# Sample rows of the six token-major units as fp32 products with the raw weights, in four groups of 32 weight columns

## What is computed

```python
h = _rmsnorm(x, norm_g)                       # (tokens, 1024)
proj = jnp.einsum('btd,de->bte', h, w_in)     # w_in is (1024, 4608)
qa, ka, va, ga, xb, gb, qc, kc, vc, gc = jnp.split(proj, SPLIT_IDX, axis=-1)
oa, s_new = _retention(qa, ka, va, s0)        # 4 heads, chunks of 128 tokens
ob, h_new, conv_new = _rglru(xb, ...)         # width-4 convolution, then a linear recurrence
oc = attention(rmsnorm(qc), rmsnorm(kc), vc)  # window of 128, sample rows against a cache
mixed = concat[rmsnorm(oa) * silu(ga), ob * silu(gb), oc * silu(gc)]
y = x + mixed @ w_out                         # w_out is (1536, 1024)
```

## Time and profile before

| | |
|---|---|
| median of the runs | 698.38 us (3 runs, 698.27 to 698.42) |
| the profiled execution | 698.62 us |
| its span, first to last instruction | 696.8 us |
| mean granted clock of TensorE | 1.000 |
| PE busy | 688.7 us, 99% |
| PEld busy | 667.9 us, 96% |
| DVE busy | 291.9 us, 42% |
| ACT busy | 264.6 us, 38% |
| POOL busy | 106.1 us, 15% |
| DMA engines | 78 GB/s over the span |

### The profile page before, as it was taken

The page is one execution under the profiler, slowest core; times in us unless marked ns, Lnnn a source line. Parts: engine busy times, 40 slices in busy tenths (PEclk is TensorE's granted clock), DMA queues, the critical chain, the costliest instruction groups (busy, mean ns, idle before and its releaser), DMA issues.

```text
span 696.8 us, 11812 instructions
## 1 busy us (share of the span) xinstructions
PE 688.7 (99%) x4662; PEld 667.9 (96%) x4662; DVE 291.9 (42%) x645; ACT 264.6 (38%) x656; POOL 106.1 (15%) x231
## 2 busy tenths in 40 slices
PE   8999999999999999999999999999999999999998
PEld 8999999999999999999999999899899999999998
DVE  6311452343335439875532465227533662500000
ACT  7473242323232353667526554335543560200000
POOL 0002260535353000000002321122100000000000
PEclk9999999999999999999999999999999999999999
DMA  8912105122121211101041010121001351522220
GB/s 302 390 44 92 61 2 211 32 66 61 64 62 58 79 51 60 40 23 61 1 145 67 11 62 1 72 75 62 1 1 61 122 182 32 166 75 64 65 65 35
DMA packets 28146, 54.41 MB, mean 78 GB/s; under 512 B 2520, under 2 KB 20440, under 8 KB 25884
## 3 DMA queue, kind: packets, MB, share of 16 engines
q1 hardware_dynamic: 28092, 53.65, 22.9%
HBM read 46.56 MB, written 9.12 MB: 80 GB/s over the span
## 4 chain that ended last, share of the span: by engine, by line
PE 95%; ACT 1%; DVE 1%; DMA 1%; issue 1%; POOL 0%; SPq 0%; DVEq 0%
PE proj L417 22%; PE proj L419 21%; PE proj L418 21%; PE branch L419 4%; PE branch L418 4%; PE branch L417 4%; PE branch L588 2%; PE branch L653 2%; PE branch L630 2%; PE branch L504 1%; PE branch L521 1%; PE branch L536 1%; PE branch L542 1%; PE branch L643 1%; PE branch L524 1%; DMA mixed<-x_T 1%
## 5 line engine op out<-in xcount | busy, mean ns | idle before, releaser
L417 PE MATMUL proj<-big 128*128 128x352 f32 (+1 forms) x952 | 305.7, 321 | 1.9 <-DVE big L1147 1.9
L418 PE MATMUL proj<-big 128*128 128x352 f32 (+1 forms) x952 | 290.7, 305 | 0.0
L419 PE MATMUL proj<-big 128*128 128x352 f32 (+1 forms) x952 | 290.7, 305 | 0.0
L417 PEld LDWEIGHTS proj<-big 128*128 128x128 f32 x952 | 179.3, 188 | 5.7 <-ACT big L811 2.3
L418 PEld LDWEIGHTS proj<-big 128*128 128x128 f32 x952 | 179.4, 188 | 2.6 <-issue 1.9
L419 PEld LDWEIGHTS proj<-big 128*128 128x128 f32 x952 | 179.3, 188 | 0.0
L1142 DVE TENSOR_TENSOR big<-raw,big 128x512 fp32r<-128x512 f32 x72 | 48.8, 690 | 64.6 <-ACT big L805 64.6
L1570 POOL TENSOR_SCALAR stat<-stat 128x1 f32<-128x1 f32 (+2 forms) x68 | 18.0, 264 | 278.6 <-ACT junk L933 189.3
L419 PE MATMUL branch<-m_hi,big 128*128 128x352 f32 x180 | 58.0, 322 | 0.0
L418 PE MATMUL branch<-m_lo,big 128*128 128x352 f32 x180 | 58.0, 322 | 0.0
L417 PE MATMUL branch<-m_hi,big 128*128 128x352 f32 x180 | 57.9, 322 | 0.0
(11 more groups left out here) (219 smaller groups left out, 943.0 us busy)
## 6 DMA issues: line engine op xcount, KB each, us to landing
raw<-w_units SPq DMA_DIRECT2D x17, 1024.0 KB, 4.9
mixed<-x_T SPq DMA_DIRECT2D x12, 352.0 KB, 7.6
xy<-x_T SPq DMA_DIRECT2D x24, 176.0 KB, 2.4
out_y_T<-xy SPq DMA_DIRECT2D x24, 176.0 KB, 1.9
raw<-w_out SPq DMA_DIRECT2D x6, 512.0 KB, 4.1
xy<-w_out SPq DMA_DIRECT2D x6, 512.0 KB, 4.3
mixed<-x_prompt SPq DMA_DIRECT2D x5, 512.0 KB, 14.1
s<-state_ret SPq DMA_DIRECT2D x4, 512.0 KB, 3.9
```

The source lines that it names most:

```text
L417: pe.matmul(out, a_lo, b_hi, start=first, stop=False)
L418: pe.matmul(out, a_hi, b_lo, start=False, stop=False)
L419: return pe.matmul(out, a_hi, b_hi, start=False, stop=last)
```

## The change

The sample group of the six token-major units is computed in another way.

- `sample_rows(u)`, at the start of unit u: eight fp32 products, one for each k block, of the 32 sample tokens (`h_s`, the sum of the two parts) with the raw weights (`raw`). Block k goes to weight columns 32g to 32g + 31 of the array with g = k mod 4, and so to partitions 32g to 32g + 31 of `bb[4]`; the bank then holds four partial sums.
- ACT copies the bank to `hold` (`hold_copy`), ahead of slot 0.
- `sample_sum(u, out)`, where the last half of the sample group was: one fp32 product of 128 rows by 32 columns with four identities of 32 one below the other (`ident_32`, later a copy of it in `st_T[:, 0, :]`), which adds the four parts into the group's bank.
- `h_samp`, `sample_pass`, `fold_copy` and DVE's addition are gone. DVE makes `h_s` once, behind the splits of unit 1.
- `raw` is read until `sample_rows(u)` is done, so `load_w(u + 1)` waits for it (`pre_done`), and in token-major units `w_at` is (6, 8, 10, 12) in place of (3, 5, 7, 9). `load_w(16)` moves behind the loads of the second half's cache.
- Users of `bb[4]` wait for `held`; `sample_rows` of units 13 and 15 wait for the tails and for the end of the sample attention of half 0 (`smix_c`, DVE L1452, slot 15 of unit 14).

```diff
--- before.py
+++ after.py
@@ -61,7 +61,7 @@
     return NT + 1 if UNITS[u][0] in TOKEN_MAJOR else 6
 
 
-FOLDS = [u for u in range(NU) if UNITS[u][0] in TOKEN_MAJOR]
+TOKEN_UNITS = [u for u in range(NU) if UNITS[u][0] in TOKEN_MAJOR]
 FIRST_GROUP = [sum(n_groups(v) for v in range(u)) for u in range(NU + 1)]
 GROUPS = [(u, j) for u in range(NU) for j in range(n_groups(u))]
 
@@ -126,7 +126,8 @@
             return big[:, a + part * D:a + (part + 1) * D]
 
 
-        h_samp = sb("h_samp", [P, KD, 2 * NS], F32R)
+        h_s = sb("h_s", [P, KD, NS])
+        hold = sb("hold", [P, UNIT])
         raw = sb("raw", [P, wsz])
         ident = sb("ident", [P, P])
         ones = sb("ones", [P, P])
@@ -168,13 +169,13 @@
             o_sq = sb("o_sq", [P, P], scope=r)
             o_rs = sb("o_rs", [P, 2, NS], scope=r)
             erow = sb("erow", [P, NS], scope=r)
+            ident_32 = sb("ident_32", [P, 32], scope=r)
         with ExitStack() as r:
 
             sb("mixed_s", [P, 3 * H, TOK], scope=r)
             sb("under_v", [P, 2 * (NT + 1) * UNIT + N_CR], scope=r)
             xt = sb("xt", [P, 3, D], scope=r)
             dgs = sb("dgs", [P, NT + 1, 32], scope=r)
-            ident_32 = sb("ident_32", [P, 32], scope=r)
         with ExitStack() as r:
             sb("mixed_b", [P, 3 * H, TOK], scope=r)
             XW = 3 + SEQ + DB * 7
@@ -216,8 +217,8 @@
             w0_in0 w0_in1 w0_in2 w0_in3 x_in0 x_in1 x_in2 x_in3 x_in4 x_in5 x_in6 x_in7 x_in8 x_in9 x_in10 x_in11
             xt_in0 xt_in1 xt_in2 xt_in3 xt_in4 xt_in5 xt_in6 xt_in7 xt_in8 x_again0 x_again1 x_again2 wo_in0 wo_in1 wo_in2 wo_in3
             stored_cache stored_ret stored_tails stored_kv stored_y0 stored_y1 stored_y2
-            ones_set h_hi_set h_lo_set hs_set sq_set e9_set rcol_set ecol_set diag_set spread rb_set
-            row_set gate_set ga_set ga_silu w_hi_set w_lo_set proj_done act_freed fold_set folded
+            ones_set h_hi_set h_lo_set hs_set pre_done held sq_set e9_set rcol_set ecol_set diag_set spread rb_set
+            row_set gate_set ga_set ga_silu w_hi_set w_lo_set proj_done act_freed
             scores_done kturn_done masked kdec_set qdec_set vsel_set o_done kv_done kv2_done s_set s2_set
             o_ss o_pow o_ms o_root o_set oT_done mix_a
             lam_exp decay_set conv_set gates_done gates_read exp_set m2_set m_set
@@ -269,6 +270,8 @@
                 if u > 0:
                     sp.wait_ge(S_["w_hi_set"], PIECES * u)
                     sp.wait_ge(S_["w_lo_set"], PIECES * u)
+                if u - 1 in TOKEN_UNITS:
+                    sp.wait_ge(S_["pre_done"], TOKEN_UNITS.index(u - 1) + 1)
                 sp.dma_start(raw[:], io["w_units"][u]).then_inc(S_["raw_in"], 16)
 
             def load_cache(half):
@@ -328,6 +331,7 @@
             for u in range(9, 13):
                 load_w(u)
             sp.wait_ge(S_["lru_set"], H)
+            sp.dma_start(st_T[:, 0, :], io["c_ident_32"]).then_inc(S_["ident_32_in"], 16)
             sp.dma_start(cc[:], io["c_att"][:, 0:N_CC]).then_inc(S_["cc_in"], 16)
             load_cache(0)
             load_w(13)
@@ -343,6 +347,7 @@
                     sp.dma_start(cc[:, C_BIAS:N_CC], io["c_att"][:, N_CC:N_CC + 4 * P]).then_inc(S_["cc_in"], 16)
                     sp.wait_ge(S_["sav_done"], 1)
                     load_cache(1)
+                    load_w(16)
 
                 for t in (NT - 1, NT):
                     n9 = 9 * half + t
@@ -356,8 +361,6 @@
                         store(io["s_k"][b, WINDOW - DS:WINDOW, half], kn[rows, n9 % 2, :], "stored_kv")
                         store(io["s_v"][b, WINDOW - DS:WINDOW, half], v_c[rows, half, t, :], "stored_kv")
                 load_w(15 + 2 * half)
-                if half == 0:
-                    load_w(16)
 
             sp.wait_ge(S_["w_hi_set"], PIECES * NU)
             sp.wait_ge(S_["w_lo_set"], PIECES * NU)
@@ -394,7 +397,8 @@
         SILU_AT = {(7, 3): 0, (7, 4): 1, (10, 4): 2, (10, 5): 3, (12, 4): 4, (12, 5): 5, (12, 6): 6, (12, 7): 7}
 
         def w_at(u):
-            return (2, 3, 4, 5) if u == 7 else (0, 1, 2, 3) if 8 <= u <= 11 else (3, 5, 7, 9)
+            return (2, 3, 4, 5) if u == 7 else (0, 1, 2, 3) if 8 <= u <= 11 else \
+                (6, 8, 10, 12) if u in TOKEN_UNITS else (3, 5, 7, 9)
 
         def att_slot(u, s):
 
@@ -418,15 +422,28 @@
                 pe.matmul(out, a_hi, b_lo, start=False, stop=False)
                 return pe.matmul(out, a_hi, b_hi, start=False, stop=last)
 
-            def sample_pass(out, a, b_hi, b_lo, first, last):
-
-
-                if first:
-                    pe.matmul(out[0:2 * NS, :], a, b_hi, start=True, stop=False)
-                mm = pe.matmul(out[0:NS, :], a[:, 0:NS], b_lo, start=False, stop=False)
-                if not first:
-                    mm = pe.matmul(out[0:2 * NS, :], a, b_hi, start=False, stop=last)
-                return mm
+            def sample_rows(u):
+
+                pe.wait_ge(S_["raw_in"], 16 * u)
+                if u == TOKEN_UNITS[0]:
+                    pe.wait_ge(S_["hs_set"], 1)
+                if u == TOKEN_UNITS[3]:
+                    pe.wait_ge(S_["tails_copied"], 1)
+                if u == TOKEN_UNITS[5]:
+                    pe.wait_ge(S_["smix_c"], 1)
+                for k in range(KD):
+                    g = k % 4
+                    mm = pe.matmul(bb[4][32 * g:32 * g + NS, 0:UNIT], h_s[:, k, :], raw[:, k * UNIT:(k + 1) * UNIT],
+                                   start=(k < 4), stop=(k >= 4))
+                mm.then_inc(S_["pre_done"], 1)
+
+            def sample_sum(u, out):
+
+                i = TOKEN_UNITS.index(u)
+                if i in (0, 2):
+                    pe.wait_ge(S_["ident_32_in"], 16 if i == 0 else 32)
+                pe.wait_ge(S_["held"], i + 1)
+                return pe.matmul(out, ident_32[:] if i < 2 else st_T[:, 0, :], hold[:], start=True, stop=True)
 
             def first_unit():
                 pe.wait_ge(S_["ones_set"], 1)
@@ -455,6 +472,7 @@
             def spread_scale():
 
                 pe.wait_ge(S_["diag_set"], 1)
+                pe.wait_ge(S_["held"], 1)
                 for r in range(4):
                     rows = slice(32 * r, 32 * r + 32)
                     pe.matmul(bb[1 + r][:, 0:32 * NT], ones[rows, :], dgs[rows, 0:NT, :].rearrange("p t n -> p (t n)"),
@@ -477,7 +495,8 @@
                         cols = chunk_cols(j)
                         w = [w_part(u % 2, i)[:, k * UNIT:(k + 1) * UNIT] for i in range(2)]
                         if j == NT:
-                            mm = sample_pass(bank[:, 0:UNIT], h_samp[:, k, :], w[0], w[1], k == 0, k == KD - 1)
+                            if k == KD - 1:
+                                mm = sample_sum(u, bank[0:NS, 0:UNIT])
                             continue
                         mm = three_pass(bank[0:n, 0:UNIT], h_hi[:, k, cols], h_lo[:, k, cols], w[0], w[1],
                                         k == 0, k == KD - 1)
@@ -560,6 +579,8 @@
                     pe.wait_ge(S_["o_set"], m + 1)
                     if m > 0:
                         pe.wait_ge(S_["mix_a"], m)
+                    if m == 0:
+                        pe.wait_ge(S_["held"], 2)
                     pe.transpose(bb[4][:, 0:P], o_nrm[:, m % 2, :], ident[:]).then_inc(S_["oT_done"], 1)
                 else:
                     pe.wait_ge(S_["o_ss"], m + 1)
@@ -591,6 +612,7 @@
             def turn_tails():
                 pe.wait_ge(S_["lru_set"], H)
                 pe.wait_ge(S_["gates_read"], 24)
+                pe.wait_ge(S_["held"], 3)
                 for f in range(H):
                     mm = pe.transpose(bb[4][0:36, f * P:(f + 1) * P], tails[:, f, :], ident[:])
                 mm.then_inc(S_["tails_turned"], 1)
@@ -662,6 +684,7 @@
             def samp_scores(half, part):
 
                 if part == 0:
+                    pe.wait_ge(S_["held"], 5 + half)
                     pe.wait_ge(S_["qT_set"], 9 * half + 9)
                     pe.wait_ge(S_["kcache_in"], 16 * (half + 1))
                     if half == 0:
@@ -734,8 +757,6 @@
                         ret_one(base + s)
                 if (u, s) == (2, 3):
                     spread_scale()
-                if (u, s) == (2, 15):
-                    pe.wait_ge(S_["hs_set"], 2)
                 if (u, s) in LRU_AT["gates"]:
                     lru_gates(LRU_AT["gates"][u, s])
                 if (u, s) == TAILS_AT:
@@ -750,6 +771,8 @@
 
             first_unit()
             for u in range(1, NU):
+                if u in TOKEN_UNITS:
+                    sample_rows(u)
                 for j in range(n_groups(u)):
                     for half in range(2):
                         group_half(u, j, half)
@@ -837,16 +860,12 @@
                 bank = proj_bank(FIRST_GROUP[16] + e)
                 act.activation(bank[:, 0:CH], bank[:, 0:CH], ACT.Silu).then_inc(S_["ga_silu"], 1)
 
-            def fold_copy(u):
-
```

(33 more changed lines are left out.)

## The result

The changed kernel takes 702.33 us (median; five executions from 702.06 to 703.22) against 698.40 for the kernel before (six executions, 698.15 to 698.79): the ratio is 1.0058, with a 95% interval of 1.0046 to 1.0069. The profiled execution took 702.06 us, with a span of 700.3 us.

What follows compares the result with a forecast made beforehand. PE's own instruction list was taken to set the time. 4 x 0.12 + 2 x 1.20 + 0.65 - 0.3 - 0.4 = +2.8 us gave 701.2 us (+0.4%), range 698.8 to 706.6.

Steps and rivals of the forecast that it cites:

- Column groups abreast: In sample_rows, four column groups stream at once, so eight products take 0.85 us plus 0.02 stagger, against 3.41 in a row.
- 1.20 us for a visit of the rows: sample_rows at a unit's start: 0.33 us for the visit to 32 columns plus 0.87 for the products.
- 0.75 for the sum against 1.83: sample_sum costs 0.33 for its visit plus 0.43, where the removed sixteen sample-pass products took 1.83 us.
- +0.12 in unit 2: Rows and sum together 1.95 us against 1.83 removed: +0.12 each in units 2, 3, 13 and 15, +0.5 in all.
- The wait at turn_k(7): Slot 17, units 12 and 14: PE still waits for group 7's norm, so rows are paid in full, +1.20 each.
- The moved splits: Unit 14: a split ahead of samp_probs in DVE's slot 9, +0.65 us; unit 12: splits leave slots where ACT is late, -0.3.
- L643's wait gone: From unit 13 into 14, the old copy and addition no longer hold up ACT's L986: -0.4 us.
- SP's queue harmless: load_w(u+1) starts with unit u, lands 4.9 us later, at least 8 us before its first reader: no cost.
- The failed step: Slot 17, units 13 and 15: the queries' norm comes out even, covered by slot 16's attention products; no cost counted.

Runs made afterwards that it cites:

- e1: Changed kernel with all eight products of sample_rows in one column group, other rows of hold zero: 718.29 us, ratio 1.0284 to the kernel before.
- e2: Changed kernel with the eight products of sample_rows alternating between two column groups: 707.46 us, ratio 1.0133 to the kernel before.
- e5: Changed kernel with the sum on all 128 columns of the identity, leaving out the adding of the four parts: 701.37 us, ratio 1.0039.
- e6: Changed kernel with unit 14's splits at slots 3, 5, 9 and 11 of ACT, one later on DVE: 702.55 us, by time inconclusive.
- e7: Kernel before with only the splits moved, to slots 6, 8, 10 and 12 in the six token-major units: 698.74 us beside 698.65.
- e4: Changed kernel with the sum moved from ahead of slot 17 to ahead of slot 16: 700.96 us, ratio 1.0036 to the kernel before.
- e8: e4 plus the next token-major unit's rows right behind the sum (units 3, 13, 14, 15): 698.04 us beside 698.65 for the kernel before.
- e9: e8 and e6 together, on the changed kernel: 697.54 us, ratio 0.9983 to the kernel before at 698.68 us.
- e3: Changed kernel with neighbouring blocks in one column group (0 and 1 in group 0, and so on): 702.42 us, ratio 1.0059.

## Why the prediction was right, and where it was not

- **Column groups abreast: right.** Most of the forecast hung on this choice, and e1 and e2 bear it out (3.57, 1.85, 1.00 us).
- **1.20 us for a visit of the rows: right.** (1,5) to (2,0) gains 1.20, (11,5) to (12,0) 1.20.
- **0.75 for the sum against 1.83: right where it stands alone.** (3,7) to (4,0) is -1.07, where -1.08 was forecast.
- **+0.12 in unit 2: wrong.** The sum of unit 2 and the rows of unit 3 follow each other in the same tiling and share one visit: (2,7) to (3,0) is -0.19 and not +0.12. I had priced each as a visit of its own (e5: taking the sum out of that visit gains nothing, elsewhere 0.3).
- **The wait at turn_k(7), +1.20 in units 12 and 14: right.** (12,7) to (13,0) is +1.19, (14,7) to (15,0) +1.23. The end of unit 14 in the changed kernel, against the earlier trace rows (rows between left out):

```profile
460.07 0.28 PE L423 MATMUL proj<-big 128*128 128x256 f32 x1
460.39 0.62 PE L446 MATMUL proj<-hold,st_T 128*32 128x256 f32 x2
461.21 0.54 POOL L1581 TENSOR_TENSOR stat<-stat 128x1 f32<-128x1 f32 x1
461.78 0.35 DVE L1376 SCALAR_TENSOR_TENSOR kn<-proj,stat,gain 128x128 f32<-128x128 f32 x1 [3.28 <-POOL stat L1581]
462.19 0.33 PE L631 MATMUL branch<-ident,kn 128*128 128x128 f32 x1 [1.18 <-DVE kn L1376]
```

  2.12 us from the group's last product to the turn, before and after; the rows come behind it, not over it.
- **The moved splits: right in unit 14** (+0.65 forecast, +0.6 by e6), **and in unit 12 more than forecast** (-0.47 from (12,0) to (12,7), and the same in e7; forecast -0.3). The prediction read 0.3 out of the earlier trace rows, which show 0.2; either is less than what the wait costs from start to start.
- **L643's wait gone, and SP's queue harmless: right.** In the kernel before the turn of the probabilities starts 1.28 us behind the scores of slot 0 in unit 14 (422.15 to 423.43), in the changed one 0.86 (424.56 to 425.42): -0.42, where -0.4 was forecast. No wait of PE names a DMA.
- **The failed step:** "The queries' norm in slot 17 of units 13 and 15 comes out even: the attention's products of slot 16 cover it." Slot 17 did come out even, but this looked only at the reader in slot 17 and not at slot 16 itself. Slot 16's scores need ACT's copy of the queries that PE turned one slot earlier, 0.80 us from L641's start to L985's end, and the half sample pass between the slots was their cover. The table puts the loss at 0.8 us in each of the two units: (13,7) to (14,0) is +0.51 where -0.28 was forecast, (15,0) to (16,0) is -0.28 where -1.08 was. The sum that e4 lays over it takes back 0.7 of each. It was in no term of the prediction's sum.

Forecast +2.8. Less 0.3 for the shared visit and 0.2 in unit 12, plus 1.6 for the two waits: +3.9, against 3.95 by the table. The 1.6 is read from the same table; e4 on its own shows 1.4 of it. The forecast of 701.2 was 1.1 us low: the failed step alone would have made it 1.6 low, and two terms that were too high happened to give 0.5 back.

## What to carry over

A piece of work on the bound engine is also the cover of every latency that runs under it: before it is taken out or moved, go through each slot from it to the next and ask of each operand how long ago it was started, not only of the reader that looks latest. Here the removed sample passes covered four such latencies, two turns of keys (1.1 us each more than the 0.12 of the other units) and two of queries (0.8 each). Together they are 3.8 of the 3.95 us: without them the change would have come out about even. Small-column fp32 products are cheap when spread over column groups, and their price is the visit, so put them side by side; and where a latency is bare, put them over it (e8, e9).

## What was not expected of the hardware

Passes of different column groups did not start in the program's order. In the changed kernel the sum of unit 2 (L446, column group 0) runs while the rows of unit 3 (L436) have already begun in the other groups, before its own second pass (products only):

```profile
78.56 0.40 PE L446 MATMUL proj<-hold,ident 128*32 128x256 f32 x1
78.57 0.42 PE L436 MATMUL branch<-raw,h_s 128*32 128x256 f32 x3
78.80 0.38 PE L446 MATMUL proj<-hold,ident 128*32 128x256 f32 x1
```

Three products that stand behind the sum in the program start 0.01 us after its first pass and 0.23 before its second. e3 agrees: with two neighbours in each group, sixteen passes take 1.02 us, as with the groups in turn, where passes in the program's order would have taken about 2.1 by the estimate made for it.
